# Expert weights split by one 128x2048 operation per chunk and engine instead of two of 128x1024

## The reference, cut to what matters

```python
def moe_swiglu(xn, w_router, we_gate, we_up, we_down):     # xn (1,256,1024)
    logits = (xn @ w_router).astype(jnp.float32)
    top_v, top_i = lax.top_k(logits, TOP_K)                # TOP_K = 2
    top_w = jax.nn.softmax(top_v, axis=-1)
    gates = jnp.sum(jax.nn.one_hot(top_i, N_EXPERTS) * top_w[..., None], axis=-2)
    y = jnp.zeros_like(xn)
    for e in range(N_EXPERTS):                             # 8 experts, hidden width 3584
        y = y + gates[..., e:e + 1] * swiglu(xn, we_gate[e], we_up[e], we_down[e])
    return y
```

## Time and profile before

| | |
|---|---|
| median of 3 runs | 1424.89 us (1424.01 to 1428.08) |
| the profiled execution | 1425.73 us, its span 1424.0 us |
| PE busy | 1405.5 us, 99% |
| DVE busy | 1188.1 us, 83% |
| ACT busy | 1040.3 us, 73% |
| granted TensorE clock, mean | 0.996 |
| experts' part | about 480 us to the end |

### The profile page before, as it was taken

One profiled execution on the slowest core, in us unless ns is written; L12 is line 12 of the kernel. 1 busy time (PEld: TensorE's weight loads), 2 busy tenths in 40 slices (PEclk: granted clock), 3 DMA queues, 4 the chain that ended last, 5 costly groups with the idle time before them and its releaser, 6 DMA issues.

```text
span 1424.0 us, 18990 instructions
## 1 busy us (share of the span) xinstructions
PE 1405.5 (99%) x6803; PEld 1173.9 (82%) x6803; DVE 1188.1 (83%) x1545; ACT 1040.3 (73%) x1367; POOL 87.8 (6%) x107
## 2 busy tenths in 40 slices
PE   9999999999999999999999999999999999999998
PEld 8998888888897878888888878888878888887886
DVE  6968654454588699999899999989999998999996
ACT  6666544444478587887888897788888878889785
POOL 1000000000010100000000030000004000003000
PEclk9999999999999999999999999999999999999999
DMA  9554555555163599999999999999999999999994
GB/s 308 160 191 151 185 198 184 196 179 187 50 227 112 188 359 397 376 373 380 381 356 388 401 409 398 403 382 389 394 404 398 409 395 365 384 403 402 406 402 160
DMA packets 143063, 442.60 MB, mean 311 GB/s; under 512 B 8862, under 2 KB 20476, under 8 KB 142972
## 3 DMA queue, kind: packets, MB, share of 16 engines
q1 hardware_dynamic: 139772, 429.89, 80.2%
q0 software_dynamic: 3168, 11.54, 2.8%
q10 hardware_dynamic: 32, 0.01, 0.0%
HBM read 433.54 MB, written 7.86 MB: 310 GB/s over the span
## 4 chain that ended last, share of the span: by engine, by line
PE 89%; DVE 9%; ACT 1%; issue 0%; POOL 0%; DVEq 0%; POOLq 0%; ACTq 0%
PE bank L587 85%; DVE w_lo L1945 6%; PE bank L1231 1%; DVE xT_lo L2628 1%; PE bank L932 0%; DVE act_f L2669 0%; PE bank L599 0%; DVE xT_lo L1989 0%; ACT w_hi L1394 0%; PE bank L607 0%; PE bank L1195 0%; DVE aT_hi L2679 0%; PE bank L1084 0%; ACT kS L1696 0%; ACT vS L1696 0%
## 5 line engine op out<-in xcount | busy, mean ns | idle before, releaser
L1945 DVE TENSOR_TENSOR w_lo<-raw,w_hi 128x1024 fp32r<-128x1024 f32 (+2 forms) x832 | 952.0, 1194 | 130.4 <-ACT w_hi L1394 125.5
L1394 ACT ACTIVATE w_hi<-raw 128x1024 fp32r<-128x1024 f32 (+2 forms) x832 | 836.3, 1043 | 229.7 <-PE bank L587 191.8
L587 PE MATMUL bank<-w_hi,xT_hi 128*128 128x512 f32 (+3 forms) x1358 | 527.1, 388 | 2.5 <-issue 1.1
L587 PE MATMUL bank<-w_hi,xT_lo 128*128 128x512 f32 (+3 forms) x1358 | 520.9, 384 | 0.0
L587 PE MATMUL bank<-w_lo,xT_hi 128*128 128x512 f32 (+3 forms) x1358 | 520.0, 383 | 0.0
L587 PEld LDWEIGHTS bank<-w_hi,xT_hi 128*128 128x128 f32 x1358 | 255.1, 188 | 52.6 <-issue 3.3
L587 PEld LDWEIGHTS bank<-w_hi,xT_lo 128*128 128x128 f32 x1358 | 255.0, 188 | 48.9
L587 PEld LDWEIGHTS bank<-w_lo,xT_hi 128*128 128x128 f32 x1358 | 255.3, 188 | 46.1
L587 PE MATMUL bank<-w_hi,aT_hi 128*128 128x512 f32 x544 | 217.2, 399 | 4.9 <-DVE w_lo L1945 4.9
L587 PE MATMUL bank<-w_lo,aT_hi 128*128 128x512 f32 x544 | 214.9, 395 | 0.0
L587 PE MATMUL bank<-w_hi,aT_lo 128*128 128x512 f32 x376 | 148.7, 395 | 0.0
(11 more groups left out here) (391 smaller groups left out, 753.5 us busy)
## 6 DMA issues: line engine op xcount, KB each, us to landing
raw<-in_we_gate_dram SPq DMA_DIRECT2D x112, 1024.0 KB, 8.3
raw<-in_we_up_dram SPq DMA_DIRECT2D x112, 1024.0 KB, 8.9
raw<-in_we_down_dram SPq DMA_DIRECT2D x112, 1024.0 KB, 9.4
raw<-in_w_gate_dram SPq DMA_DIRECT2D x14, 1024.0 KB, 5.1
raw<-in_w_up_dram SPq DMA_DIRECT2D x14, 1024.0 KB, 5.1
raw<-in_w_down_dram SPq DMA_DIRECT2D x14, 1024.0 KB, 4.8
raw<-in_w_in_dram SPq DMA_DIRECT2D x16, 768.0 KB, 5.4
raw<-in_w_out_dram SPq DMA_DIRECT2D x8, 1024.0 KB, 5.7
```

The lines of the kernel that those rows point to most:

```text
L587: return pe.matmul(o, a, b, start=start, stop=stop, skip_group_check=True, **kw)
L1394: act.activation(split_piece(w_hi, c, shape, half), raw_piece(c, shape, half), ACT.Copy).then_inc(hi_ready, 1)
L1945: dve.tensor_tensor(split_piece(w_lo, c, shape, half), raw_piece(c, shape, half), F(split_piece(w_hi, c, shape, half)), ALU.subtract).then ...
```

## The change

In the experts' part ACT and DVE split a chunk by one operation of 128x2048 each. The two pieces of a chunk lie beside each other in the ring (2c % 6 is 0, 2 or 4), and `both_pieces` joins them. The operation raises its counter by 2. ACT now waits until both slots of the chunk are free: `piece_used` at 2c - 4, where the first piece alone needed 2c - 5. The subtraction waits for the high part of the whole chunk. What stands between the pieces stands between chunks now, so at odd places one piece is moved past it: on ACT down piece 28 ahead of `e_high` moves behind it (`pieces(24, 29)` becomes `chunks(12, 14)`), and piece 33 behind the second `e_high` moves ahead of it (`chunks(14, 17)`); on DVE pieces 28, 32 and 36 move likewise, the last of them behind `e_product` (`pieces(33, 37)` becomes `chunks(16, 18)`). PE and SP are not changed: PE still waits and counts piece by piece. The first two chunks of unit 0 on ACT, and the first three on DVE, are still split by pieces, as is all ahead of the experts.

```diff
+        def both_pieces(t, c):
+            p = 2 * c % SPLIT_SLOTS
+            return t[:, p:p + 2, :].rearrange("p s n -> p (s n)")
...
+            def chunk_high(j, more, lap):
+                c = C_MOE + j
+                act.wait_ge(raw_here[c % RAW_SLOTS], 16 * (c // RAW_SLOTS + 1) + 16 * lap)
+                act.wait_ge(piece_used, 2 * c + 2 - SPLIT_SLOTS + 2 * more)
+                act.activation(both_pieces(w_hi, c), raw[:, c % RAW_SLOTS, :], ACT.Copy).then_inc(hi_ready, 2)
...
-                pieces(4, 13)
+                chunks(2, 6)
                 keep_gate(u)
                 act.wait_ge(sem("turned"), u + 1)
                 e_silu(C_MOE + 4, more, None, 2)
-                pieces(13, 24)
+                chunks(6, 12)
                 for i in range(WIDE - 1):
                     m, lp = more + WIDE_STEP * i, lap + 2 * i
-                    pieces(24, 29, m, lp)
+                    chunks(12, 14, m, lp)
                     e_high(t0 + 2 * i, 0, narrow)
                     e_silu(C_MOE + 12, m, n0 + 2 * i + 2, 2)
-                    pieces(29, 33, m, lp)
+                    chunks(14, 17, m, lp)
                     e_high(t0 + 2 * i + 1, 1, narrow)
-                    pieces(33, 48, m, lp)
-                p, n, t = 2 * SMALL, n0 + NF - 3, t0 + NF - 3
-                pieces(p + 8, p + 9)
+                    chunks(17, 24, m, lp)
+                c, n, t = SMALL, n0 + NF - 3, t0 + NF - 3
                 e_high(t, 0, narrow)
                 e_silu(C_MOE + SMALL + 2, more, n + 2, 1)
-                pieces(p + 9, p + 14)
+                chunks(c + 4, c + 7)
                 e_high(t + 1, 1, narrow)
-                pieces(p + 14, p + 18)
+                chunks(c + 7, c + 9)
                 for b in range(2):
                     act.wait_ge(sem("eaT_half_psum"), 2 * u + b + 1)
                     high_part(2 * b, 2, B[(6, 7)[b]], narrow).then_inc(sem("eaT_half_hi"), 1)
                 if not last:
                     gathered(u + 1)
-                pieces(p + 18, p + 20)
+                chunks(c + 9, c + 10)
                 if not last:
-                    for j in range(4):
-                        split_high(p0 + 2 * FFN_CHUNKS + j, UP, more, lap)
+                    chunks(FFN_CHUNKS, FFN_CHUNKS + 2)
...
+            def chunk_low(j, more):
+                c = C_MOE + j
+                dve.wait_ge(hi_ready, 2 * c + 2 + 2 * more)
+                dve.tensor_tensor(both_pieces(w_lo, c), raw[:, c % RAW_SLOTS, :], F(both_pieces(w_hi, c)),
+                                  ALU.subtract).then_inc(lo_ready, 2)
...
-                    pieces(24, 29, m)
+                    chunks(12, 14, m)
                     e_low(t0 + 2 * i, 0, narrow)
-                    pieces(29, 33, m)
+                    chunks(14, 16, m)
                     e_low(t0 + 2 * i + 1, 1, narrow)
-                    pieces(33, 37, m)
+                    chunks(16, 18, m)
                     e_product(C_MOE + 16, m, n0 + 2 * i + 2, 2)
-                    pieces(37, 48, m)
+                    chunks(18, 24, m)
...
                 e_low(t, 0, narrow)
-                pieces(p + 8, p + 13)
+                chunks(c + 4, c + 6)
                 e_product(C_MOE + SMALL + 4, more, n + 2, 1)
                 e_low(t + 1, 1, narrow)
-                pieces(p + 13, p + 17)
+                chunks(c + 6, c + 8)
                 for b in range(2):
                     dve.wait_ge(sem("eaT_half_hi"), 2 * u + b + 1)
                     low_part(2 * b, 2, B[(6, 7)[b]], narrow).then_inc(sem("eaT_half"), 1)
-                pieces(p + 17, p + 18)
+                chunks(c + 8, c + 9)
                 if not last:
                     gathered(u + 1)
-                pieces(p + 18, p + 20)
+                chunks(c + 9, c + 10)
```

More of the change, by code:

```diff
@@ L1848, in unit, with chunks @@
                 more, lap, n0, t0 = FFN_CHUNKS * u, NF * u, NF * u, (NF - 1) * u
-                p0 = 2 * C_MOE
-                def pieces(a, b, m=more, lp=lap):
+                def chunks(a, b, m=more, lp=lap):
                     for j in range(a, b):
-                        split_high(p0 + j, WROW, m, lp)
-                pieces(4, 13)
+                        chunk_high(j, m, lp)
+                chunks(2, 6)
                 keep_gate(u)
@@ L2688, in unit, with chunks @@
                 more, n0, t0 = FFN_CHUNKS * u, NF * u, (NF - 1) * u
-                p0 = 2 * C_MOE
                 first = u == 0
-                def pieces(a, b, m=more):
+                def chunks(a, b, m=more):
                     for j in range(a, b):
-                        split_low(p0 + j, WROW, m)
-                pieces(6, 8)
+                        chunk_low(j, m)
+                chunks(3, 4)
                 if first:
                     rank_experts()
-                pieces(8, 10)
+                chunks(4, 5)
                 if first:
                     order_units()
-                pieces(10, 12)
+                chunks(5, 6)
                 if first:
                     unit_products()
-                pieces(12, 14)
+                chunks(6, 7)
                 if first:
                     unit_tables()
-                pieces(14, 21)
+                chunks(7, 10)
                 e_product(C_MOE + 8, more, n0, 2)
-                pieces(21, 24)
+                chunks(10, 12)
                 if not last:
@@ L2745, in unit @@
                     return
-                for j in range(6):
-                    split_low(p0 + 2 * FFN_CHUNKS + j, UP, more)
+                chunks(FFN_CHUNKS, FFN_CHUNKS + 3)
             gathered(0)
```

## The result

The changed kernel takes 1463.32 us (median of four runs, 1462.50 to 1464.08) against 1424.61 us: ratio 1.0268, 95% interval 1.0256 to 1.0281. It is slower by 38.7 us; forecast were 42.8 by the sum and 1468 as the time.

A forecast was written before the change was run, and what follows sets the result against it. PE was taken to set the time, DVE close behind in narrow units. Stalls of 24.3 us in narrow units, 13.6 in full units and 4.9 at the ends sum to 42.8, giving 1468 us; own range 1453 to 1483, overall 1443 to 1488.

The forecast's parts named there:

- The operations: Whole-chunk split: 1.90 us for ACT's copy, 2.285 for DVE's subtraction; a chunk saves 0.11 us of ACT, 0.07 of DVE.
- The hops: Waits in the hand-over: PE to ACT 0.19 us, ACT to DVE 0.04, DVE to PE 0.14; whole hand-over 4.55 us.
- The narrow step: Steps of narrow units: PE stalls 2.6 us a step, 1.7 of it at chunk 18 behind DVE's product.
- The full step: Steps of full units: small PE stalls at chunks 14, 16 and 18, 0.6 us a step.
- The tail of a full unit: End of a full unit: chunk 40 0.15 us late, chunk 41 1.5 behind the gathered rows, sum 1.6.
- The hand-over behind a full tail: Behind each tail but the last: `y_out` costs 0.4 us at chunk 44, silus 0.2 at the next unit's chunk 6.
- The narrow tail and the hand-over to a full unit: Narrow tail: PE 4.4 us late where it was 2.0, 2.3 more; plus 0.6 for the hand-over behind it.
- Raw slots and transfers: SP's fetches of raw chunks become 0.5 us tighter against PE; costed at nothing.
- C: Rival: cover holds and DVE has less to do in the narrow tails, 2.3 us faster, 1423 us; chance 0.07.
- D: Rival: the operation runs as two, or DVE's saving and PE's stalls cancel; 1425 us, no change; chance 0.04.
- A: Rival: only the narrow units lose, full steps and hand-overs stall nowhere; 1450 us; chance 0.16.
- B: Rival: counter's 2 or longer operation adds 0.1 to 0.2 us a hop, late transfers add more; 1487 us; chance 0.16.

The follow-up runs named there:

- e2: ACT copies whole chunks in the changed kernel's order, DVE subtracts by pieces in the order of the kernel before; 1448.41 us, ratio 1.0160 to the kernel before.
- e3: ACT copies by pieces in the order of the kernel before, DVE subtracts whole chunks in the changed kernel's order; 1443.55 us, ratio 1.0137 to the kernel before.
- e11: Changed kernel with a split ring of four chunks and most work between chunks on ACT and DVE one chunk later; 1429.64 us, ratio 1.0033 to the kernel before.
- e4: Changed kernel with DVE's product behind chunk 18 instead of ahead of it; 1466.48 us, ratio 1.0296 to the kernel before.
- e5: Changed kernel with a split ring of four chunks instead of three in the experts' part, same operations and order; 1458.20 us, ratio 1.0239 to the kernel before.
- e7: Changed kernel with 18 identity transposes on PE ahead of chunk 41 in the narrow units; 1462.39 us, ratio 1.0261 to the kernel before.

## Why the prediction was right

Direction, mechanism and size held: 1468 was forecast, 1463.3 measured, inside the forecast's own range of 1453 to 1483. That the sum came within 4 us is in part luck, since the tails of the full units were priced 5 us too high and the hand-overs behind the tails 4 us too low. Both traces hold the same 6803 matmuls in the same order, so the delay of each chunk can be read from start to start. By the steps of the prediction:

- **The operations:** right, 1921 and 2287 ns against 1900 and 2285.
- **The hops:** DVE to PE is 0.14 us as before. ACT to DVE grew: a copy that starts at 774.88 and takes 1.92 is followed at 776.90, 0.10 us, where it was 0.04 in the earlier trace rows. I had costed this at zero with 0.1 allowed, for the counter that goes up by 2. ACT's counter is not it: in e2 ACT raises it by 2 and DVE follows 0.03 us behind (775.76 + 1.92 to 777.71), in e3 by 1 and DVE follows after 0.10 (771.08 + 1.06 to 772.24). What goes with the longer hop is that DVE's wait became an instruction of its own, the DVEq L1952 of the chain above, one for each of the 333 whole subtractions (count: shortest, median, longest in ns, first and last start):

```profile
L1952 DVEq EVENT_SEMAPHORE  x333: 21/21/1715, 491.7 to 1445.4; - x167
```

  e3 has as many; the kernel before and e2 have 5 ahead of its subtractions in the whole span. Whether the 2 on DVE's own counter makes it so, no run shows.
- **The narrow step:** 2.3 and 2.8 us by the distances of the transposes (765.32, 798.31, 825.83 against 761.67, 792.33, 817.06), 5.1 for the two where 5.2 was forecast. The place was right too, chunk 18 behind the product. Only chunk 20 was off, 0.1 late in the first step and 0.4 in the second for 0.5.
- **The full step:** 0.4 and 0.5 us, forecast 0.6.
- **The tail of a full unit:** this term was mis-sized: 1.6 us, four times, where it was 0.2 to 0.3. Alone it would have made the forecast 5 us too high. I had chunk 41 late by 1.5 us and chunk 40 by 0.15; from start to start PE's first matmul of chunk 41 is 0.2 late. The hop was wrong: "ACT starts 0.19 us after PE begins the matmuls behind the released chunk". Between chunks 37 and 38 PE has transposes to do, and the slot is free when they begin, not when they end. The changed kernel's PE and ACT there:

```profile
718.51 0.60 PE L1242 MATMUL bank<-ident,act_f 128*128 128x128 f32 x4
718.95 1.04 PE L1199 MATMUL bank<-ident,xg 128*128 128x128 f32 x8
719.74 0.48 PE L591 MATMUL bank<-w_hi,aT_hi 128*128 128x512 f32 x1
```
```profile
718.79 1.92 ACT L1392 ACTIVATE w_hi<-raw 128x2048 fp32r<-128x2048 f32 x1 [0.88 <-PE bank L591]
```

  The copy of chunk 40 starts 0.95 us ahead of chunk 38's matmuls; I had it 0.19 behind them, 1.1 us too late for all that follows in the tail.
- **The hand-over behind a full tail:** mis-sized the other way, which took back 3 us (and 1 more behind the narrow tails): 0.4 at chunk 44 and 0.2 at chunk 6 forecast, 1.3 measured, of it 0.7 at chunks 44 and 45 of this unit and 0.6 at 6, 7 and 11 of the next. PE at chunk 44 behind unit 1:

```profile
737.30 0.47 PE L591 MATMUL bank<-w_hi,xT_hi 128*128 128x512 f32 x1 [0.39 <-DVE w_lo L1953]
```

- **The narrow tail and the hand-over to a full unit:** forecast 2.9 us, measured 5.1 and 4.0 less 0.9 for that unit's own steps, so 4.2 and 3.1. In unit 3 some 1.5 us of it are the clock (below), and behind unit 6 another 1.1, which I had not in the sum.
- **Raw slots and transfers:** right at nothing. Before, ACT waited 17.1 us for up, 9.0 for gate and 9.0 for down transfers; in the changed kernel no wait of ACT for a transfer stands in the list of waits from 520 us on. That a slower PE asks for less is the likely reason: in e11, where PE is quick again, waits of ACT for up and gate transfers are back, 12.8 and 9.2 us.

Of the rivals, C (cover holds) and D are out. A is wrong on the full units, which lose 2.5 us where it had them lose nothing, but the narrow ones do take most: by the table 20 us in the three narrow units and 7 more where two of their tails reach into the next unit. B's added hop is there at 0.06 us, inside the range.

## What to carry to other kernels

In a ring between engines, the cover is (number of slots less one) times what the last engine takes for a slot, less the whole hand-over; making the unit of hand-over twice as large in the same memory raised the hand-over from 2.65 to 4.6 us and cut what hides it from five pieces to two chunks. Price all that stands between the hand-overs on each engine against that cover, at the stage where the last engine is quickest. And where an engine works through a fixed list, a larger ring is of use only if the list lets the engine run ahead.

## What the runs showed that was not expected

**The clock after a gap.** In the tails of two of the three narrow units, 2 and 6, PE ran at half its rate behind the gap ahead of chunk 41. Unit 2 of the changed kernel, PE's timeline, then the same stretch by busy time (us, busy us and counts by engine, granted clock, DMA share, GB/s):

```profile
846.23 0.55 PE L591 MATMUL bank<-w_hi,aT_hi 128*128 128x512 f32 x1 [2.17 <-DVE w_lo L1953]
846.57 0.63 PE L591 MATMUL bank<-w_lo,aT_hi 128*128 128x512 f32 x1
847.00 0.63 PE L591 MATMUL bank<-w_hi,aT_hi 128*128 128x512 f32 x1
```
```profile
846.20:849.60 3.40, 3.37 (x9) 2.65 (x10) 3.40 (x2) 0.00 (x0) 0.00 (x0) 0.54 1.00 382
1086.90:1089.10 2.20, 2.10 (x9) 1.42 (x9) 2.20 (x2) 0.07 (x1) 0.00 (x0) 1.00 1.02 363
```

Matmuls start every 0.43 us instead of 0.233, the granted clock is 0.54, that is nearly all of the stretch at 1.2 GHz. Before the fall PE had been idle for 2.17 us in a stretch that already held a gap of 0.56. The same gap in unit 4 (second line) left the clock at 1.00, and e4 had a gap of 2.17 us in unit 2 without a fall. In unit 6 the clock was 0.69 from 1326.40 to 1330.00. The traces of the other runs bear this out. Over all runs, these two included, there are 20 narrow tails in which PE waits 1.89 to 2.17 us ahead of chunk 41. Behind 13 of these waits the clock fell (behind all three in e2 and in e5), behind 7 it did not, and behind none of the shorter ones, 1.66 us and less. The gap of 0.56 is not needed: e2 and e3 have none ahead of chunk 40 and the clock fell there too. So a gap of this length can bring the clock down and need not. From chunk 41 to chunk 44 PE takes 9.38 us in unit 2 and 9.00 in unit 6, against 7.95 in unit 4: the two falls cost 1.4 and 1.1 us.

With the gap filled (e7) PE's wait there is 0.19 us and the clock in the same tail is 1.00:

```profile
845.61 2.13 PE L611 MATMUL bank<-ident 128*128 128x128 f32 x18
847.93 0.47 PE L591 MATMUL bank<-w_hi,aT_hi 128*128 128x512 f32 x1 [0.19 <-DVE w_lo L1955]
```
```profile
846.50:850.00 3.50, 3.31 (x20) 2.42 (x18) 3.50 (x3) 1.32 (x1) 0.00 (x0) 1.00 1.01 359
```

Unit 3 of e7 takes 121.85 us where the changed kernel took 123.34, the 1.5 us that the fall had cost; e4, whose clock held in unit 2 as well, has 121.87. Units 5 are alike, 122.21 and 122.24: there the clock had not fallen. One profiled execution of each run shows this. Over the whole run it is worth 2.5 to 3 us, so the clock, one of the rivals, has only that part of the 38.7. In the two profiled executions PE's last matmul comes 0.8 us earlier in e7 (1453.87 against 1454.70) though its expert products began 1.9 later (486.79 against 484.92); what follows that matmul took 1.5 us longer there (7.6 against 6.1), and the medians differ by 0.9, less than the runs can tell.
